# Gate one-hots of the PEER stage: one compare-and-multiply per token and term on VectorE instead of wide compares, wide multiplies and ScalarE's third term

## What is computed

```python
v1, i1 = lax.top_k(s1, PEER_TOPK)
v2, i2 = lax.top_k(s2, PEER_TOPK)
...
sc, pos = lax.top_k(comb, PEER_TOPK)
e1 = jnp.take_along_axis(i1, pos // PEER_TOPK, axis=-1)
e2 = jnp.take_along_axis(i2, pos % PEER_TOPK, axis=-1)
experts = e1 * N_KEYS + e2
gate = jax.nn.softmax(sc, axis=-1)
ue = u[experts]
act = jax.nn.gelu(jnp.einsum('thkd,td->thk', ue, xt).astype(jnp.float32), approximate=False) * gate
return jnp.einsum('thk,thkd->td', act.astype(xt.dtype), v[experts])
```

## Time and profile before

| what | value |
|---|---|
| median of 3 runs | 4504.73 us (4504.63 to 4519.54) |
| profiled execution: span, first to last instruction | 4504.3 us, 0.4 us under the median |
| TensorE busy | 4205.9 us, 93% of the span |
| VectorE busy | 3126.5 us, 69% |
| ScalarE busy | 1558.1 us, 35% |
| GpSimd busy | 1504.4 us, 33% |
| gate stage | about 2536 to 3060 us of the span |
| tail | about 3060 to 3425 us |

### The profile page before, as it was taken

The page is one execution under the profiler, slowest core; times in us unless marked ns, Lnnn a source line. Parts: engine busy times, 40 slices in busy tenths (PEclk is TensorE's granted clock), DMA queues, the critical chain, the costliest instruction groups (busy, mean ns, idle before and its releaser), DMA issues.

```text
span 4504.3 us, 63924 instructions
## 1 busy us (share of the span) xinstructions
PE 4205.9 (93%) x22555; PEld 3573.1 (79%) x22555; DVE 3126.5 (69%) x6090; ACT 1558.1 (35%) x2721; POOL 1504.4 (33%) x1221
## 2 busy tenths in 40 slices
PE   7999999999899799989999999898798999999998
PEld 4668877777688578779889998898797888888886
DVE  7531037777477644459999788885467998888888
ACT  4221135556477533232222444442121222222222
POOL 0000000000044311003888788887853222222220
PEclk9999999999999899999999999999899999999999
DMA  6647323333456465233444699999898888888885
GB/s 263 244 168 248 127 84 128 114 126 121 155 175 203 133 214 186 85 110 88 83 80 94 156 264 264 265 274 275 219 338 303 299 307 288 286 288 285 286 289 196
DMA packets 479090, 913.42 MB, mean 203 GB/s; under 512 B 188675, under 2 KB 269971, under 8 KB 475269
## 3 DMA queue, kind: packets, MB, share of 16 engines
q1 hardware_dynamic: 321380, 509.42, 34.7%
q0 software_dynamic: 151136, 363.35, 27.0%
q10 hardware_dynamic: 6336, 37.75, 2.3%
HBM read 747.37 MB, written 188.17 MB: 208 GB/s over the span
## 4 chain that ended last, share of the span: by engine, by line
PE 26%; DVE 11%; POOL 10%; DMA 5%; issue 4%; SPq 1%; ACT 0%; DVEq 0%; ACTq 0%; POOLq 0%
PE ph_gate_ps L2482 15%; PE ph_hid_ps L2482 7%; POOL scratch_scattered L2357 5%; POOL ph_ring L2363 4%; DMA ph_ring<-in_u_rows,held_tiles 4%; PE ph_hid_ps L2407 3%; PE ph_hid_ps L2397 1%; DVE ph_hot L2669 1%; DVE ph_hot L2676 1%; DVE ph_ring L2781 1%; DVE ph_u_lo L2614 1%; DVE ph_score L2641 1%; DVE ph_index L2643 1%; DVE ph_index L2640 1%; DVE ph_placef L2679 1%
## 5 line engine op out<-in xcount | busy, mean ns | idle before, releaser
L2357 POOL DMA_INDIRECT scratch_scattered<-held_tiles x384 | 709.2, 1847 | 289.5 <-DVEq L2704 155.6
L2407 PE MATMUL ph_hid_ps<-ph_n_hi,ph_u_hi 128*128 128x384 f32 x2048 | 709.6, 346 | 67.8 <-DVE ph_u_lo L2614 67.8
L2407 PE MATMUL ph_hid_ps<-ph_n_lo,ph_u_hi 128*128 128x384 f32 x2048 | 700.2, 342 | 0.0
L2407 PE MATMUL ph_hid_ps<-ph_n_hi,ph_u_lo 128*128 128x384 f32 x2048 | 699.2, 341 | 0.0
L2383 POOL DMA_INDIRECT ph_ring<-in_v_experts,ph_pick_again x256 | 240.6, 940 | 778.4 <-DVE held_tiles L2887 743.4
L2781 DVE CUSTOM_DVE_ANT_0 ph_ring<-ph_ring,ph_n_rows 128x1024 f32<-128x1024 f32 x256 | 309.4, 1224 | 212.8 <-DMA ph_ring<-in_u_rows,held_tiles 212.0
L2407 PEld LDWEIGHTS ph_hid_ps<-ph_n_hi,ph_u_hi 128*128 128x128 f32 x2048 | 397.2, 194 | 75.5 <-DVE ph_u_lo L2614 75.2
L2407 PEld LDWEIGHTS ph_hid_ps<-ph_n_lo,ph_u_hi 128*128 128x128 f32 x2048 | 396.9, 194 | 0.2
L2407 PEld LDWEIGHTS ph_hid_ps<-ph_n_hi,ph_u_lo 128*128 128x128 f32 x2048 | 396.4, 194 | 0.0
L2363 POOL DMA_INDIRECT ph_ring<-in_u_rows,held_tiles x256 | 329.3, 1286 | 152.3 <-DVE held_tiles L2781 90.2
L2887 DVE SCALAR_TENSOR_TENSOR held_tiles<-ph_ring,ph_factor,held_tiles 128x1024 f32<-128x1024 f32 x254 | 324.7, 1278 | 0.0
(11 more groups left out here) (396 smaller groups left out, 9853.0 us busy)
## 6 DMA issues: line engine op xcount, KB each, us to landing
ph_u_raw<-in_tiles SPq DMA_DIRECT2D x136, 512.0 KB
ph_v_raw<-in_v_experts SPq DMA_DIRECT2D x124, 512.0 KB, 4.8
scratch_hidden<-ph_hidden SPq DMA_DIRECT2D x128, 384.0 KB, 4.3
ph_u_raw<-scratch_hidden SPq DMA_DIRECT2D x124, 384.0 KB, 4.9
proj_w_ch<-in_w_ch SPq DMA_DIRECT2D x49, 512.0 KB, 3.7
mb_w_raw<-in_w_branch POOLq DMA_DIRECT2D x48, 512.0 KB, 3.9
scratch_gate_tiles<-ph_gates SPq DMA_DIRECT2D x48, 512.0 KB
ph_hidden<-scratch_gate_tiles SPq DMA_DIRECT2D x124, 192.0 KB, 3.9
```

Of the source, the lines that this page charges most:

```text
L2357: pool.indirect_dma_start(d["scattered"], bass.IndirectOffsetOnAxis(place_of[:, at:at + 1], 0), held[:, 2, GM + at:GM + at + 1], None, com ...
L2407: mm = pe.matmul(hid_halves[r][:, c, :], u[r][a][:, k, :], n2[b][:, k, c * CUT:(c + 1) * CUT], start=(k == 0 and a + b == 0), stop=(k == K ...
```

## The change

The column one-hots and the two wide multiplies are gone. For each token VectorE makes the row one-hot with one `tensor_scalar` (compare) and each of the three scaled column one-hots with one `tensor_scalar` (compare, then multiply), all 128 elements long, from a bf16 copy of the column numbers 0 to 127 (`iota_b`), with scalars that are columns of `chosenT` and of the shares. The three shares are kept in f32 in slab 0 of `held_tiles` (and slab 2 of `chosenT`), rounded to bf16 values. ScalarE's third term and the semaphores `col_ready` and `third_ready` are gone.

```diff
-        col_hot = [in_held(0, b) for b in range(NBANK)]
+        share = [held[:, 0, n * HALF:n * HALF + GM] for n in range(2)] + [chosenT[:, 2, :]]
...
                         pe.wait_ge(hot_ready[b], j + 1)
                         pe.wait_ge(gates_taken[b], j + 1)
-                        pe.wait_ge(third_ready[b], j + 1)
...
                     for r in range(2):
-                        for b in (2 * r, 2 * r + 1):
-                            act.wait_ge(col_ready[b], j + 1)
-                            for t in range(TOK):
-                                ins = act.activation(term[2][b][:, t, :], col_hot[b][:, t, :], ACT.Copy,
-                                                     scale=chosenT[:, 2, bass.ds(j * PER_STEP + (b * TOK + t), 1)])
-                            ins.then_inc(third_ready[b], 1)
                         take_hidden(r, m, m - 1 if r == 0 else m - 7)
...
+                own.of(dve.tensor_copy(iota_b[:], iota[:]))
                 for n in range(2):
-                    own.of(dve.tensor_copy(share[n][:], chosenT[:, 2, :]))
+                    own.of(dve.tensor_copy(rounded[:], share[2]))
                     own.wait()
-                    own.of(dve.tensor_tensor(chosenT[:, 2, :], chosenT[:, 2, :], share[n][:], ALU.subtract))
+                    own.of(dve.tensor_copy(share[n], rounded[:]))
+                    own.of(dve.tensor_tensor(share[2], share[2], rounded[:], ALU.subtract))
                     own.wait()
...
                         dve.wait_ge(gates_mm[b], j + 1)
-                        toks = slice(j * PER_STEP + b * TOK, j * PER_STEP + (b + 1) * TOK)
-                        dve.tensor_tensor(row_hot[b][:], iota[:].unsqueeze(1).to_broadcast([P, TOK, NK]),
-                                          chosenT[:, 0, toks].unsqueeze(2).to_broadcast([P, TOK, NK]), ALU.is_equal)
-                        dve.tensor_tensor(col_hot[b], iota[:].unsqueeze(1).to_broadcast([P, TOK, NK]),
-                                          chosenT[:, 1, toks].unsqueeze(2).to_broadcast([P, TOK, NK]), ALU.is_equal).then_inc(col_ready[b], 1)
-                        dve.wait_ge(col_ready[b], j + 1)
-                        for n in range(2):
-                            ins = dve.tensor_tensor(term[n][b], col_hot[b], share[n][:, toks].unsqueeze(2).to_broadcast([P, TOK, NK]), ALU.mult)
+                        for t in range(TOK):
+                            at = j * PER_STEP + b * TOK + t
+                            dve.tensor_scalar(row_hot[b][:, t, :], iota_b[:], chosenT[:, 0, at:at + 1], None, ALU.is_equal)
+                            for n in range(3):
+                                ins = dve.tensor_scalar(term[n][b][:, t, :], iota_b[:], chosenT[:, 1, at:at + 1], share[n][:, at:at + 1],
+                                                        ALU.is_equal, ALU.mult)
                         ins.then_inc(hot_ready[b], 1)
```

More of the change, by code:

```diff
@@ L2087, in stage_peer_topk @@
         iota = sp.sb("iota", [P, NK])
+        iota_b = sp.sb("iota_b", [P, NK], BF16)
         hid_ps = [sp.ps(f"hid_ps{r}", [P, S]) for r in range(2)]
@@ L2119, in stage_peer_topk @@
             row_hot = [gates_sb(f"row_hot{b}", [P, TOK, NK], BF16) for b in range(NBANK)]
-            share = [gates_sb(f"share{n}", [P, GM], BF16) for n in range(2)]
+            rounded = gates_sb("rounded", [P, GM], BF16)
             gates = [gates_sb(f"gates{s}", [P, NK, GATE_TOK]) for s in range(2)]
@@ L2180, in stage_peer_topk @@
         share_step = sp.sem("share_step")
-        col_ready = [sp.sem(f"col_ready{b}") for b in range(NBANK)]
         hot_ready = [sp.sem(f"hot_ready{b}") for b in range(NBANK)]
-        third_ready = [sp.sem(f"third_ready{b}") for b in range(NBANK)]
         gates_mm = [sp.sem(f"gates_mm{b}") for b in range(NBANK)]
@@ L2557, in step @@
                 def step(k, s, x):
-                    j = 8 * k + (4 * s + x)
                     m = GATE_TILE0 // 2 + 8 * k + (4 * s + x)
                     for r in range(2):
-                        for b in (2 * r, 2 * r + 1):
-                            act.wait_ge(col_ready[b], j + 1)
-                            for t in range(TOK):
-                                ins = act.activation(term[2][b][:, t, :], col_hot[b][:, t, :], ACT.Copy,
-                                                     scale=chosenT[:, 2, bass.ds(j * PER_STEP + (b * TOK + t), 1)])
-                            ins.then_inc(third_ready[b], 1)
                         take_hidden(r, m, m - 1 if r == 0 else m - 7)
@@ L2571, in step @@
                         for b in (2 * r, 2 * r + 1):
-                            act.wait_ge(gates_mm[b], j + 2)
+                            act.wait_ge(gates_mm[b], 8 * k + (4 * s + x) + 2)
                             act.activation(gates[s][:, :, x * PER_STEP + b * TOK:x * PER_STEP + (b + 1) * TOK],
```

## The result

| what | before | after |
|---|---|---|
| median of 8 runs, us | 4505.05 (4501.15 to 4519.54) | 4526.02 (4516.20 to 4531.83) |
| ratio to before, 95% interval | – | 1.0039 (1.0026 to 1.0051) |
| profiled span, us | 4504.3 | 4525.2 |
| up to the first one-hot | 2533.7 | 2537.3 |
| gate stage, first to end of last one-hot | 523.5 | 539.7 |

The change costs 0.39% or 17.6 us (0.0039 x 4505; the medians themselves lie 21.0 us apart). That is inside the forecast range and on its side, at a third of the +50 forecast, and under the 0.5% that the prediction called "same". The span is 1.7 us under its own run (4526.87), where the opening table took 0.4 from a single difference; it does not enter the comparison.

What follows compares the result with a forecast made beforehand. GpSimd's queue was taken to bound the gate stage. VectorE's 530 us of work plus 45 of collisions and 5 of waits gave 580, +56; casts +1, tail -7: 4504.7 + 50 = 4555 us, range 4508 to 4625.

Steps and rivals of the forecast that it cites:

- same: Whole kernel: a time within about 0.5%, 22 us, which a measurement cannot tell from no change; chance 0.15.
- The bound before: Gate stage: GpSimd's queue sets the pace at 10.9 us a half step, with VectorE close behind at 9.6 us.
- The price of a bank: VectorE, one bank of one-hots: from 2.53 us to 3.33, the middle between 2.80 and 3.87 us.
- VectorE's work: Gate stage: one-hots 320, `low` 54 and dot products 156 us, together 530 against 453 before.
- The bound passes to VectorE: Gate stage: VectorE at 580 us exceeds GpSimd's 500, so the stage grows by 56 us; chance 0.72.
- The collisions: Gate stage: some 150 GpSimd DMAs fall into one-hot runs and delay VectorE 0.30 us each, 45 us; ends 0 and 53.
- GpSimd enters the tail with its four buffers full where it now enters just in time: Tail behind the gate stage: GpSimd is two scatter and gather pairs ahead, -7 us.
- GpSimd waiting for dot products: Gate stage, a sign in the profile after: this wait, 19 us before, grows by some 60 us.
- GpSimd's DMAs get longer or shorter by more than 0.2 us: A sign in the profile after: such a shift on average would make the forecast wrong.
- faster rival: Gate stage: cheaper one-hots and shorter GpSimd DMAs without wide two-input compares, stage about 480 us, -44, 4461 us; chance 0.07.
- GpSimd stays the bound: Gate stage: a bank under about 3 us and absorbed collisions keep 524 us; 4505 us, chance 0.15.
- Starved: Gate stage: one-hot runs stop GpSimd preparing DMAs, stage 758 us, +234, 4739 us; chance 0.06.

Runs made afterwards that it cites:

- f32_columns: The changed kernel with the one-hots reading the f32 column numbers instead of the bf16 copy: 4582.92 us, 1.0161 of before.
- two_terms_on_scalar: The changed kernel with ScalarE making the second and third terms, VectorE the row, a plain column and one scaled one-hot: 4501.73 us, 0.9983 of before.
- wide_third: The kernel before with the third term made by a third wide multiply on VectorE instead of ScalarE's activations: 4524.73 us, 1.0037 of before.

## Why the prediction was right and wrong, step by step

**The bound before: right.** "GpSimd's queue sets the pace": with half of its DMAs out of the stage, the stage lost 60 us. That TensorE's wait for the third term and ScalarE's 123 us are worth nothing holds as far as seen: TensorE's wait only changed its releaser, 41 us for ScalarE to 66 us for L2789.

**The price of a bank: right.** Forecast 3.33 us, the middle between 2.80 and 3.87, measured 3.34. The starts are 0.163 us apart behind a one-scalar one-hot and 0.223 behind a two-scalar one, and 4 x 0.163 + 12 x 0.223 = 3.33. The elements' part shrank with the bytes of the input. The prediction's estimate by the fourfold rate of the Trainium skill (VectorE: DVE Perf Modes, § Mode 4×_2P — both tricks at once) was 3.32 us, and the trace agrees with 3.34. At the upper end, f32_columns's undisturbed starts were at 0.196 and 0.256 us, as the rows of L471 and L514 had said.

**VectorE's work: right.** Forecast 320 + 54 + 156 = 530 us, measured 321.0 + 53.5 + 155.8 = 530.3. "The bound passes to VectorE": right, by the gathers' wait (61 to 6 us, forecast 5) and the chain.

**The collisions: the step that failed.** "150 x 0.30 = 45 us" was mis-sized; it measured 1 us. 530.0 + 6.3 of waiting for gathers + 3.4 of other gaps is the stage of 539.7, and the forecast 580 was the same work, 5 of waits and 45 more. The 0.30 us had been read from durations: the row of L2698, 181 against 434 ns. A duration shows that an instruction ended later, not that the next began later, and the row behind L2698 in the same timeline of before already told the two apart. Without and with a scatter beside it:

```profile
2091.65 0.18 DVE L2699 TENSOR_SCALAR ph_expert<-ph_expert 128x48 int32<-128x48 int32 x1
2091.97 0.20 DVE L2701 CAST held_tiles<-ph_split_id 128x48 int32 x1
```
```profile
2151.68 0.37 DVE L2699 TENSOR_SCALAR ph_expert<-ph_expert 128x48 int32<-128x48 int32 x1
2152.19 0.20 DVE L2701 CAST held_tiles<-ph_split_id 128x48 int32 x1
```

L2699 starts 0.09 us behind L2698 (2091.56 and 2151.59) in both. Only L2701, which idles until the two before it are done, starts later, 0.51 us behind L2699 and not 0.32. Between one-hots nothing waits for an end. They do get longer by up to 0.37 us (676 against a median of 307 ns), and their starts hardly move. In f32_columns the starts move, and all of its 1536 one-hots lose 16 us by it, still a third of the 45. Why the delay is absorbed at the higher rate and not at the lower was not tried. Two smaller faults of the same term: its share of the time (320 / 580) was taken from its own result, and the upper end of the sum has 55 us for it where the text had worked out 53.

**"GpSimd enters the tail with its four buffers full where it now enters just in time": wrong, and small.** At the end of the stage 138 gathers were issued for 135 finished dot products before, and 139 for 135 after: three ahead before, four now. One gather ahead is under 2 us, and 7 were credited; the tail shows no gain at all.

**GpSimd waiting for dot products "by some 60 us more": it was 13.** GpSimd's own time stayed at 499 us, with longer scatters and shorter gathers, so it could wait only as much longer as the stage grew, 16 us and not the forecast 56. "GpSimd's DMAs get longer or shorter by more than 0.2 us" did not come about (+0.11 and -0.07), so the prediction stood by its own test; but it had left out that they move at all. The faster rival rested on just this: no wide two-input compares beside the scatters. The prediction held that no row of before shows that contention; its trace does, in the 29 scatters of 2.02 us in the table. That half of the rival happened (29 scatters held up by 512-element instructions before, none after), and was undone by the other half: GpSimd, now paced by the dot products, starts more scatters just behind the beginning of a dot product or `low`, 39 where there were 8, and each of those costs 1 us more and not 0.45. That the new pacing is what moved the starts is argued, not tried.

**The rivals.** *GpSimd stays the bound* fell (VectorE idle 10 us, not 61), but its time, 4505, is nearer to the result than was comfortable. *Faster* needed a bank under 2.53 us (16 starts of 158 ns); two_terms_on_scalar, which has 2.22 us,, gained 8 us, not 44, since the gather and scatter pair stayed at 3.6 us. *Starved* fell: scatters beside one-hots last 1.58 us, as undisturbed ones do.

**The chances.** The text had both ends of the collisions, 0 and 53 us, and gave "slower by more than 0.5%" all of the 0.72 "except a sliver". But its own sum with the lower end is 530 + 5 = 535, so +11 + 1 - 7 = +5 us: in the class "same". A bound from below that was judged possible should have carried chance into that class. The measured +0.39% lies there.

## What to carry to other kernels

When work is put on an engine with some slack beside the bounding queue, what it costs is the new work less the slack, and the slack can be had from the trace: here 77 us of work for 16 us of stage. That holds only while the queue's own work stays what it was; wide_third cost as much with 58 us of work. Read the cost of contention from start to start in a row of instructions that follow closely; a longer duration alone is no cost. And an engine's price per DMA is not its own: at equal VectorE work, 509 and 511 us, the stage was 14.5 us shorter with one-input instructions, because a GpSimd DMA that begins under a two-input one waits it out.

## What the runs showed of the hardware that was not expected

- A GpSimd scatter takes 1.58 us if VectorE runs a one-input instruction when it starts, 2.02 to 2.08 us behind a two-input one of 0.68 us that has just begun, and 2.55 to 2.62 us behind one of 1.22 us. Exceptions are scatters just ahead of a dot product that follows without a gap: 2.67 us, 15 times in two_terms_on_scalar. It is the moment of the start that counts, so two engines that wait for each other may lock into a costly phase.
- A one-hot of 128 bf16 elements lengthens from 0.31 to as much as 0.68 us beside a GpSimd DMA, while the run of them loses 1 us in the whole stage. With f32 input, starts move by up to about 0.2 us.
- Two-input bf16 instructions of 512 elements lasted 688 ns with the element varying innermost against a broadcast scalar, and 418 to 420 ns with four tokens innermost.
- Bf16 matmuls whose operands stood four elements apart lasted 298 ns and not 224.
